# Two norm seams and the last stage of a hybrid retention, RWKV-7 and PEER block rebuilt

## What is computed

```python
def rms_norm(x, w):
    y = xf * lax.rsqrt(jnp.mean(xf * xf, axis=-1, keepdims=True) + NORM_EPS)
    return (y * w.astype(jnp.float32)).astype(x.dtype)
...
h = rms_norm(x, norm1_w[layer])
z = h @ w_in[layer]
...                       # retention and RWKV-7 heads, gates, two branch projections
x = x + merged @ w_out[layer]
h2 = rms_norm(x, norm2_w[layer])
x = x + peer(h2, peer_w_q[layer], ..., peer_u[layer], peer_v[layer])
return rms_norm(x, final_norm_w)
```

## Time and profile before

| | us |
|---|---|
| three runs | 2739.16, 2739.53, 2745.03 |
| median | 2739.53 |
| the profiled execution | 2744.74 |
| its span in the trace | 2742.9 |
| PE busy in it | 2609.2 (95%) |
| DVE, ACT, POOL busy | 1724.4, 1255.1, 812.2 |

### The profile page before, as it was taken

How to read it: one execution, slowest core, us unless ns; L and a number is a source line. 1 busy time by engine, 2 the same in 40 slices (tenths; PEclk the granted TensorE clock), 3 DMA queues, 4 the chain that set the end, 5 groups by cost and what they waited for, 6 DMA issues and landing times.

```text
span 2742.9 us, 56869 instructions
## 1 busy us (share of the span) xinstructions
PE 2609.2 (95%) x18602; PEld 2459.9 (90%) x18602; DVE 1724.4 (63%) x2830; ACT 1255.1 (46%) x2259; POOL 812.2 (30%) x612
## 2 busy tenths in 40 slices
PE   7989988888999998899999999999999999999997
PEld 6989977888899998899999999999998888888885
DVE  4467964333564664557986577777766666666665
ACT  5446532222444444544444644444345555555554
POOL 0020114333000000028998877777740000000000
PEclk9999999999999999999999999999999999999998
DMA  6655540000466556555555554555555555666665
GB/s 184 180 166 161 172 122 16 1 0 0 138 177 176 163 177 184 145 170 180 180 178 169 167 168 154 159 160 154 160 177 191 193 193 196 191 192 194 192 194 184
DMA packets 334371, 429.16 MB, mean 156 GB/s; under 512 B 26853, under 2 KB 299607, under 8 KB 332631
## 3 DMA queue, kind: packets, MB, share of 16 engines
q1 hardware_dynamic: 334295, 428.12, 50.9%
HBM read 423.82 MB, written 4.19 MB: 156 GB/s over the span
## 4 chain that ended last, share of the span: by engine, by line
PE 60%; issue 26%; POOL 10%; DVE 2%; ACT 1%; DMA 0%; POOLq 0%; SPq 0%; DVEq 0%; ACTq 0%
POOL w_lo L1006 9%; PE PS L341 8%; PE PS L667 8%; PE PS L668 8%; PE PS L666 8%; PE PS L342 8%; PE PS L343 8%; PE PS L630 2%; PE PS L504 1%; PE PS L468 1%; PE PS L502 1%; PE PS L493 1%; DVE w_lo L1020 1%; PE PS L516 0%; DVE big L1205 0%
## 5 line engine op out<-in xcount | busy, mean ns | idle before, releaser
L341 PE MATMUL PS<-act_hi,w_hi 128*128 128x256 f32 x4256 | 1220.1, 287 | 32.9 <-DVE w_lo L1020 20.0
L342 PE MATMUL PS<-act_lo,w_hi 128*128 128x256 f32 x4256 | 1210.0, 284 | 0.0
L343 PE MATMUL PS<-act_hi,w_lo 128*128 128x256 f32 x4256 | 1209.7, 284 | 0.0
L1020 DVE TENSOR_TENSOR w_lo<-raw,w_hi 128x512 fp32r<-128x512 f32 x1064 | 720.9, 702 | 305.4 <-ACT w_hi L696 302.1
L1006 POOL TENSOR_TENSOR w_lo<-raw,w_hi 128x512 fp32r<-128x512 f32 x512 | 666.2, 1334 | 687.6 <-ACT w_hi L877 687.6
L341 PEld LDWEIGHTS PS<-act_hi,w_hi 128*128 128x128 f32 x4256 | 822.5, 193 | 39.4 <-issue 19.6
L696 ACT ACTIVATE w_hi<-raw 128x512 fp32r<-128x512 f32 x1064 | 637.5, 624 | 419.0 <-PE PS L343 418.1
L342 PEld LDWEIGHTS PS<-act_lo,w_hi 128*128 128x128 f32 x4256 | 822.8, 193 | 1.0 <-issue 1.0
L343 PEld LDWEIGHTS PS<-act_hi,w_lo 128*128 128x128 f32 x4256 | 822.4, 193 | 0.0
L666 PE MATMUL PS<-w_hi,act_hi 128*128 128x512 f32 x1024 | 398.4, 389 | 0.0
L667 PE MATMUL PS<-w_lo,act_hi 128*128 128x512 f32 x1024 | 398.4, 389 | 0.0
(11 more groups left out here) (235 smaller groups left out, 1688.0 us busy)
## 6 DMA issues: line engine op xcount, KB each, us to landing
raw<-in_peer_u SPq DMA_DIRECT2D x1024, 128.0 KB, 2.7
raw<-in_peer_v SPq DMA_DIRECT2D x256, 512.0 KB, 4.4
raw<-in_w_in SPq DMA_DIRECT2D x180, 512.0 KB, 3.8
raw<-in_w_out SPq DMA_DIRECT2D x32, 512.0 KB, 4.7
raw<-in_peer_w_q SPq DMA_DIRECT2D x128, 128.0 KB, 3.2
raw<-in_w_ret_branch SPq DMA_DIRECT2D x16, 512.0 KB, 3.5
raw<-in_w_rwkv_branch SPq DMA_DIRECT2D x16, 512.0 KB, 3.5
big<-in_x SPq DMA_DIRECT2D x2, 1024.0 KB, 6.2
```

Of the source, the lines that this page charges most:

```text
L341: pe.matmul(out, wh, xh, start=start, stop=False)
L342: pe.matmul(out, wh, xl, start=False, stop=False)
L343: return pe.matmul(out, wl, xh, start=False, stop=stop)
L1020: dve.tensor_tensor(w_lo[:, slot % 2, cols], raw[:, slot, cols], w_hi[:, slot % 2, cols].bitcast(f32), ALU.subtract).then_inc(S["unit_spli ...
```

## The change

- **Root table.** ACT runs a root of one dummy element (`sqrt_table`) at its start, after the `gates` stage and in the first V unit, so that the table is there when a norm asks for the root.
- **Squares by pieces.** Ahead of norm 1 ACT squares five pieces as DVE finishes adding them; the sums go to `part`, and DVE adds them up (a new reduce in `norm`).
- **Norm on two engines.** ACT scales the first token tile, DVE the second, each in two pieces of 128 x 1024; PE transposes the first half of the channels once both first pieces are there.
- **Weight inside the split.** `to_channels` is gone: `split_act` reads the transposed blocks in PSUM and multiplies by the channel weight, one channel block (128 x 256) per instruction, on both engines. For the first quarter it comes behind the first unit's weight split.
- **Keys.** The PEER keys are transposed and copied ahead of `wq`.
- **U stage.** Each transposition on DVE is two instructions, one for each half unit.
- **Tail.** The loads of x and the final weight stand ahead of the last 32 V loads. DVE adds the first output half beside V (turn 30 of 32) and multiplies it by the weight; ACT squares it in turn 31. After V the second half is added and squared in four pieces, ACT scales the first half, DVE the second, and SP makes four stores of 0.5 MB.

```diff
+        def turned(name, kc):
+            b = turned_bank(name, kc // 4, 0)
+            return PS[:, b:b + 2, (kc % 4) * P:(kc % 4 + 1) * P]
...
-                run_loop(sp, 0, BLOCKS // 4, load_v)
-
-            sp.wait_ge(S["half_used"], 2 * (V0 + BLOCKS + 60))
...
+                    run_loop(sp, 0, 24, load_v)
+
+                    sp.wait_ge(S["half_used"], 2 * (V0 + BLOCKS + 60))
+                    sp.dma_start(flat(Z(0, 16)).rearrange("p (a n) -> p a n", a=2),
+                                 x1_dram.rearrange("(a p) n -> p a n", p=P)).then_inc(S["x1_in"], 16)
+                    sp.dma_start(flat(Z(16, 24)), a["final_norm_w"].partition_broadcast(P)).then_inc(S["fw_in"], 16)
+                    with sp.Fori(24, BLOCKS // 4) as it:
+                        load_v(it)
+
             for tt in range(2):
...
+                for h in range(2):
+                    sp.wait_ge(*((S["normed"], 5 + tt) if h == 0 else (S["y_ready"], tt + 1)))
...
+            def transpose_tokens(src, done, name, nth):
+                for cg in range(4):
+                    if cg % 2 == 0:
+                        pe.wait_ge(S["normed"], 2 * nth + cg // 2 + 1)
+                        pe.wait_ge(S["normed_v"], 2 * nth + cg // 2 + 1)
+                    for tt in range(2):
+                        for c in range(4):
...
                 if name in ("main_rwkv", "wq"):
-                    act.wait_ge(S["hT" if name == "main_rwkv" else "h2T"], 5 + pc)
+                    act.wait_ge(S["xT_done" if name == "main_rwkv" else "x2T_done"], pc + 1)
+                    for kc in range(4 * pc, 4 * pc + 4):
+                        last = act.activation(act_hi[:, kc, :].rearrange("p (t n) -> p t n", t=2), turned(name, kc), ACT.Copy,
+                                              scale=channel_w(name, kc))
...
+            def sqrt_table():
+                act.activation(warm[:, 1:2], warm[:, 0:1], ACT.Sqrt)
...
+                for w in range(2):
+                    to, of = normed_views(src[0], dst[0], nth, w)
+                    act.activation(to, of, ACT.Copy, scale=rstd[:, 0:1]).then_inc(S["normed"], 1)
...
             split_seg("gates", evac_sigmoid(82), head_between)
+            sqrt_table()
             split_seg("ret")
...
+            for tt, k, at, end in ((0, 0, 0, 2), (0, 1, 2, 4), (1, 0, 0, 2), (1, 1, 2, 3), (1, 2, 3, 4)):
+                act.wait_ge(S["x1_done"], 4 * tt + end)
+                square(xs[tt][:, 512 * at:512 * end], xn[tt][:, 512 * at:512 * end], tt, k)
...
                         if h == 0 and isinstance(it, int) and it == 0 and k == 0:
                             gelu(BLOCKS // 2 - 1, 1, late=True)
+                            sqrt_table()
+                        if h == 1 and isinstance(it, int) and it == BLOCKS // 4 - 1 and k < 2:
+                            act.wait_ge(S["res_done"], k + 1)
+                            square(flat(Z(8 * k, 8 * k + 4)), flat(Z(40 + 4 * k, 44 + 4 * k)), k, 0)
...
+            for hh in range(2):
+                for tt in range(2):
+                    act.wait_ge(S["res_done"], 3 + 2 * hh + tt)
+                    square(flat(Z(8 * tt + 4 + 2 * hh, 8 * tt + 6 + 2 * hh)), flat(Z(48 + 4 * hh + 2 * tt, 50 + 4 * hh + 2 * tt)), tt, 1 + hh)
+            norm_root(2)
...
-                turned = u_part(k, 0, 8)
-                dve.transpose(turned, turned).then_inc(S["uT"], 1)
+                for hh in range(2):
+                    turned = u_part(k, 4 * hh, 4)
+                    dve.transpose(turned, turned).then_inc(S["uT"], 1)
...
+            def first_half(k):
+
+                tt = k % 2
+                x1 = flat(Z(8 * tt, 8 * tt + 4))
+                if k < 2:
...
+                else:
+                    dve.wait_ge(S["res_done"], 2)
+                    dve.tensor_tensor(flat(Z(24 + 8 * tt, 28 + 8 * tt)), x1, flat(Z(16, 20)), ALU.mult).then_inc(S["weighted"], 1)
...
+            for hh in range(2):
+                dve.wait_ge(S["half_used"], 2 * (V0 + 2 * BLOCKS) - 1 + hh)
+                for tt in range(2):
+                    x1 = flat(Z(8 * tt + 4 + 2 * hh, 8 * tt + 6 + 2 * hh))
+                    dve.tensor_tensor(x1, x1, PS[:, 4 + 2 * tt + hh, :], ALU.add).then_inc(S["res_done"], 1)
```

More of the change, by code:

```diff
@@ L682, in _ @@
         def _(act):
-            ch = Chain(act, S["act_chain"])
             def hi(m, slot, hh, first=False, stage=None):
@@ L705, in body @@
                         first = name == "main_rwkv" and isinstance(t, int) and t == 0 and j == 0 and kq < 2
-                        if name in operand and isinstance(g, int) and g == 0:
+                        ahead = name in ("main_rwkv", "wq") and kq == 0
+                        if name in operand and isinstance(g, int) and g == 0 and not ahead:
                             split_act(name, kq)
@@ L709, in body @@
                             hi(m, slot, hh, first, name)
+                        if ahead and isinstance(g, int) and g == 0:
+                            split_act(name, kq)
                         if kq == 1 and evac and not (isinstance(g, int) and g == 0):
@@ L928, in _ @@
                 else:
-                    run_loop(act, 0, BLOCKS // 4, v_hi)
-            act.wait_ge(S["res_done"], 4)
-            norm_root([flat(Z(8 * tt, 8 * tt + 8)) for tt in range(2)], [flat(Z(40, 48)), flat(Z(48, 56))], 2)
+                    run_loop(act, 0, BLOCKS // 4 - 1, v_hi)
+                    v_hi(BLOCKS // 4 - 1)
+            for hh in range(2):
[3 more added lines that the diff above has]
+            norm_root(2)
+            act.wait_ge(S["norm_rstd"], 3)
+            act.wait_ge(S["weighted"], 2)
+            for tt in range(2):
+                y = flat(Z(24 + 8 * tt, 28 + 8 * tt))
+                act.activation(y, y, ACT.Copy, scale=rstd[:, tt:tt + 1]).then_inc(S["normed"], 1)
         @block.gpsimd
@@ L1028, in body @@
                         slot = unit_slot(ku, j, kq)
-                        if name in operand and isinstance(g, int) and g == 0 and not (name == "out" and kq < 2):
+                        ahead = name in ("main_rwkv", "wq") and kq == 0
+                        if name in operand and isinstance(g, int) and g == 0 and not (name == "out" and kq < 2) and not ahead:
                             split_act(name, kq)
@@ L1057, in norm @@
                 dve.reciprocal(rstd, rstd).then_inc(S["norm_rstd"], 1)
+                if src is not None:
+                    dve.wait_ge(S["norm_rstd"], nth + 1)
+                    for w in range(2):
+                        to, of = normed_views(src, dst, nth, w)
+                        dve.tensor_scalar(to, of, rstd[:, 1:2], None, ALU.mult).then_inc(S["normed_v"], 1)
+            dve.memset(small[:, 82:88], 0.0)
+            dve.memset(warm, 1.0).then_inc(S["warm"], 1)
             dve.wait_ge(S["vecT"], 1)
```

126 lines of the change are left out of this document (67 added, 59 removed).

## The result

The changed kernel takes 2721.44 us (median of four runs, 2719.32 to 2722.40), the kernel before 2739.35 in four runs beside it (2737.03 to 2745.03). The ratio is 0.9933, 95% interval 0.992 to 0.9945. So it is faster, by 18 us. The forecast was faster, 2717 us with a range of 2710 to 2726: the sign and the range held, and the median lies 4.4 us above the forecast.

What follows compares the result with a forecast made beforehand. PE was taken as the bound, with gains only at seams where it runs dry; terms -6.5 - 10.2 - 0.4 + 1.5 + 0.7 - 0.5 + 1.5 - 8.6 = -22.5 gave 2717 us from the median 2739.5, range 2710 to 2726.

Steps and rivals of the forecast that it cites:

- First norm: Program start: first product at 21.4, 5.4 us earlier, and part of the slow clock back; gain 5.4 to 8, taken 6.5.
- Second norm and keys: Ahead of `wq`: first product 9.4 us earlier, gain 8.5 to 11.5, taken 10.2; keys' copy off the path, 0.4.
- Load behind `gates`: Behind `gates`, where PE waits for ACT: table load and dummy root (1.28 + 0.2) stand in the chain, cost 1.5.
- Load in the first V unit: First V unit: table load and dummy root delay the next `w_lo` to 2030.45 while PE frees at 2029.75, cost 0.7.
- U stage: U stage's start: first half of a transposition reaches ACT 0.6 us earlier, gain 0.5 (0 to 3); 36 us DVE hidden.
- The third rival: U stage: DVE becomes the bound; all 36 us on PE gives 2753 (chance 0.03), half gives 2735 (0.04).
- V stage: V stage: next V load behind the 3 MB lands at 13.9, wanted at 11.5; cost 1.5, range 0 to 4.
- the first rival: V stage: load behind the moved transfers 5 us or more late, then slow PE; 5 + 1.5, 2722, chance 0.13.
- the sign against it: V stage: a hole of PE above 3 us would show the forecast wrong.
- Tail: After the last matmul: first store at T + 4.1 instead of T + 12.8; gain 8.6, between 7.5 and 9.9.
- The forecast's other reading: Tail: if latency decides, the last store, issued at T + 5.5 instead of T + 15.4, sets the end; gain 9.9.
- Second and fourth rival: Seams: half of the norms' 16.7 us lost, 2725, chance 0.12; table reloaded before roots or four stores slow, 2721, 0.08.

Runs made afterwards that it cites:

- tables moved: Changed kernel with the root table behind gates loaded in the middle of out's first columns, the first V unit's behind the third: 2718.43 us, ratio 0.9923.
- the kernel with pieces and moved tables: Changed kernel with the 3 MB loaded in six 0.5 MB pieces between V loads and both root tables loaded elsewhere: 2713.35 us, again 2713.73.
- the fastest kernel: Kernel with six pieces and both root tables moved, plus ret's first operand quarters split while gates' last products run: 2709.2 us, ratio 0.9887.

## Why the prediction held, and where it was off

The signs that the forecast named came: the first product at 21.42, that of `wq` 9.4 us earlier, no table load behind V, the first store 4.1 us after the last matmul, a hole of 5.17 us behind `gates`, and one hole of PE 90 us before V's end. The median is closer to the forecast than the terms are, since one large miss, in V, is in part covered by gains that no term forecast; the end of this section adds this up.

**First norm: forecast 5.4 us and 1.1 of the clock, measured 5.4.** The start of scaling (14.15 forecast, 14.32 measured), of the transpositions (15.35, 15.57) and of the first product (21.4, 21.42) came as worked out. That the last of these agrees to 0.02 us is luck: the other kernels with the same code up to there have it at 20.6 to 21.9. DVE's piece, for which there was no row, took 0.71 us (1.42 for two), between the bounds of the nearest rows. The slow stretch of the earlier trace rows is gone:

```profile
20.00:24.00 4.00, 4.00 (x34) 4.00 (x33) 3.95 (x10) 3.85 (x10) 0.00 (x0) 1.00 0.35 119
```

What that gave is less clear. The next stage fell by 2.9 us, but by 2.5 also in the kernel in which only the loads were moved (203.9 us). Against that one 0.4 is left for the change, where the forecast had 1.1.

**Second norm and keys: forecast 10.6, measured 11.2, or 9.8 against the more usual execution.** 9.38 of it are the way from the first addition to the first product (9.4 forecast). The other 1.2 (0.8 for the clock, 0.4 for the keys) were 1.8 against before's trace, but only 0.4 against that of the kernel with the loads alone, which has the norm of before and takes 117.1 us here instead of 118.6. In that trace the clock behind the first product (1105.19) is 1.00, from 1106 to 1114; so the 0.8 for the clock is not shown as a gain of the change. The clock of 0.57 that stood behind the first product in the earlier trace rows now falls into the transpositions, and is over at the first product (1090.58):

```profile
1086.00:1090.00 4.00, 4.00 (x26) 4.00 (x25) 2.47 (x5) 3.86 (x10) 0.00 (x0) 0.64 0.14 45
1090.00:1094.00 4.00, 4.00 (x35) 3.91 (x34) 3.95 (x10) 3.78 (x10) 0.00 (x0) 1.00 0.36 91
```

**Load behind `gates`: forecast 1.5, measured 2.6.** The hole grew by 1.52 us (from 3.65 to 5.17), load and dummy root as forecast. What the step left out is the clock. From 870 to 890 there are 103 of 169 products in after, so 66 are missing, 7.8 us by 0.118 each, 2.6 beyond the hole. In before 47 are missing from 870 to 910, 5.5 us, 1.9 beyond the hole. So the slow stretch grew by 0.7. The other 0.4 us are within what two more seams exchange: ahead of `rwkv` the low clock is gone, ahead of `out` there is one now. Removing the load gave back 2.5. The Trainium skill (ScalarE: Activation LUTs, What ACT_TABLE_LOAD costs) adds a drain of 1380 ns to each switch of 1283 ns; the trace agrees with the second and shows no drain here, as the root began 1.30 us after the load.

**Load in the first V unit: forecast 0.7, measured 0.9.** The hole of 0.89 us.

**U stage: forecast 0.5, measured 0.4**, and none of it from the halves, as the kernel with whole transpositions shows (821.2). Against the kernel with the loads alone (822.9) it is 1.4; 1.2 of that is a longer slow stretch behind a hole of 3.92 us at the stage's start, with a clock of 0.70 over 10 us in that kernel and 0.84 in after. The DVE time that the halves add was mis-sized: 36 us by the prices of other operations, 15.5 measured (687 ns for a half, 1238 for a whole). The third rival, DVE as the bound of U, has fallen with it: in the stretch that answers to that of the earlier trace rows DVE stands at 73.89 of 80, and PE where it was.

```profile
1310.00:1390.00 80.00, 79.53 (x659) 78.89 (x657) 73.89 (x223) 35.51 (x67) 71.55 (x56) 1.00 0.58 179
```

**V stage: forecast 1.5, measured 6.4** (7.3 less the 0.9 of the table). This is the step that failed. The mechanism was named rightly, and the first rival had a sum of the right size, 6.5 us, but by luck: it put 5 on the late load and 1.5 on the slow clock, and they were 2.94 and 3.5. The cost lies outside the range of 0 to 4 that the step gave itself, while the sign against it, a hole above 3 us, was just missed: the sign watched the hole and not the clock behind it. Two terms of the forecast were too small. First, "the next V load lands at 13.9": counted from the V load ahead of both it landed at 15.2 (2617.21 - 2602.05), since the weight came at 13.9 and not at 12.3, and the load 1.3 behind it. The 11.3 us that the earlier trace rows show for the weight were one reading of a time that varies: from issue to landing it took 10.5 to 13.4 us in the six kernels below. With 0.7 us of PE's cover left in place of the 1.0, that made the hole 2.94 us and not 1.4. Second, no slow clock was put on it, though the first rival had one of 1.5. The six kernels with the undivided 3 MB show how that goes:

| kernel | V load landed after, us | PE's hole, us | V stage over 695.6, without the table's 0.9 |
|---|---|---|---|
| loads alone | 12.9 | 3.41 | 5.4 |
| the change | 12.4 | 2.94 | 6.4 |
| tables moved | 12.4 | 2.86 | 4.9 |
| whole transpositions | 12.1 | 2.63 | 4.8 |
| ACT alone scales | 11.6 | 2.12 | 4.3 |
| no early tables | 10.5 | 0.95 | 1.3 |

Behind each of these holes of 2.12 us or more the clock fell, which cost another 2 to 3.5 us; behind 0.95 it did not. The landing time itself varies by 2.4 us with nothing that the edits touch. By the Trainium skill (DMA: Bandwidth & Descriptors, Queues, rings and completion order) each DMA engine takes the descriptors of its ring in order. The trace agrees, with landings in the order of issue: x at 2613.5, weight at 2615.9, V load at 2617.2. It stood in the forecast as what speaks against the new place, and it was right to.

**Tail: forecast 8.6, measured 8.5.** The first store at T + 4.14 (T + 4.1 forecast), and 6.93 us from there to the end against 6.76 before. The four stores were issued 0.4 to 0.7 us apart and landed 1.3 to 1.4 us apart, the last at 2719.6: so with four stores the 2 MB bound that phase, and not the issue of the last one. The forecast's other reading, 9.9 by the last store, took the end of the issue row, 2738.75, for the last issue, which was at 2738.41.

**Second and fourth rival.** The seams did not give back: in after PE has no gap over 0.06 us from its first product to 70 us, nor from that of `wq` to 1182, so DVE's block splits held nothing up. And no root of the two norms or of the end loads its table again.

**What was not forecast: the heads, -4.4.** This part of the program is untouched. A slow stretch in it was shorter in after; the first row is of before, the second, at the same distance from the first product of the heads, of after:

```profile
428.00:432.00 4.00, 3.00 (x14) 3.01 (x15) 3.23 (x4) 0.00 (x0) 0.00 (x0) 0.50 0.00 0
```

```profile
424.00:428.00 4.00, 4.00 (x38) 4.00 (x37) 2.48 (x4) 0.00 (x0) 1.28 (x1) 1.00 0.01 4
```

The kernel with only the loads moved takes 473.6 us for this stage, so some 2.2 us of the 4.4 belong to that one execution of before; the other 2.2 it shares with all kernels that have the new first norm (471.4 to 472.0). Why these should keep the clock longer was not tried.

**Adding it up.** Against the stages of the kernel with the loads alone up to V, and of before from there on, the gains are 5.1 (first norm), 0.4 (the next stage), 2.2 (heads), -2.5 (`gates` to `out`), 9.8 (second norm), 1.4 (U), -7.3 (V) and 8.5 (end), 17.6 in all, and the medians differ by 17.9. The forecast's terms give 22.5. So V took 5.1 us more than forecast (6.4 + 0.9 against 1.5 + 0.7), `gates` 1.0, the first norm with the stage behind it 1.0 and the second 0.8, the end 0.1; the heads' 2.2 and 0.9 more in U, which nobody had worked out, hid 3.1 of these 8.0. That is luck: without it the median would be 2724.6, close to the upper end of the range of 2710 to 2726. The other end of that range is off by a little too: the terms named for it come to 2711.4, and 2.5 less for U's start is 2708.9, not 2710.

**Where the gain went.** Against before's trace the two norms and the tail gave 25.1 us, and the places of two transfers and two table loads took 9.9 back (7.3 in V, 2.6 behind `gates`). Of these 9.9 the kernel with pieces and moved tables has 8 again (2713.4 and 2713.7 against 2721.4); the second norm and the U stage, 1.9 us longer together with the table moved, hold the rest.

## What to carry to other kernels

A large transfer that is put into a prefetch ring delays the next load of the ring by nearly its whole length (3 MB made one load land after 12.4 us here, where the median is 3.9); cut it into pieces no larger than the ring's own, one between each two loads, and it costs nothing even with the DMA engines at 94%. A seam is worth rebuilding from both sides: split the next operand while the last products still run, and price a hole with the slow stretch behind it, which here was 1.6 to 3.5 us more behind most holes of 2.1 to 5.2 us. A table load belongs beside work of another engine that lasts longer than it, not at the first point where the last user is done. And a stage's gain is to be checked against the stages behind it: here 2.5 us at a seam were 0.6 by the start of V.

## What the runs showed of the hardware

- The length of a hole of PE doesn't by itself decide whether the clock falls behind it. Ahead of `rwkv` PE waits 2.61 us, and ahead of `out` 2.20, in before and after alike. In before the clock fell behind the first (0.57 from 944 to 948) and not behind the second; in after it is the other way round; and in the fastest kernel it fell behind neither. This repeats: all six traces with 3.65 us ahead of `ret` are like before, all five with 5.17 us like after, and `gates` to `out` takes 377.5 us in the ones and 379.8 to 380.0 in the others. So it goes with what stands ahead, and not by chance. Behind the second, of before and of after:

```profile
994.00:998.00 4.00, 4.00 (x36) 4.00 (x35) 3.47 (x5) 2.12 (x3) 0.00 (x0) 1.00 0.63 196
```

```profile
982.00:986.00 4.00, 4.00 (x25) 4.00 (x25) 3.14 (x5) 0.63 (x1) 0.00 (x0) 0.64 0.56 165
```

  Each is worth some 1.6 us (36 matmuls missing from 930 to 950 in before, less the 2.61; 32 from 970 to 990 in after, less the 2.20), as much as some of the terms of the forecast. Why it goes so was not settled.
- Two transpositions of 128 x 512 last 687 ns each, one of 128 x 1024 lasts 1238; but DVE is busy for only 649 ns per half (332.5 us / 512), since the next begins before the last has ended. By the single instructions 256 halvings cost 35 us (2 x 687 - 1238 = 136 ns each), by the busy time of the groups 15.5.
- DVE scales 128 x 1024 from SBUF by a value per partition in 0.71 us, ACT in 1.1 (2.19 for two).
